# Router squares taken from residual chunks, router products spread over the projection, first expert item begun on two groups, state space end reordered, first projection weights in quarters

## The chip, the cores and the metric

The kernel runs on one core of a Trainium2 chip. The metric is the device time in microseconds (us) of one execution. A run's time is a little longer than the span of its profile, which goes from the first to the last instruction on the engines. Engines are named as in the profile: PE (TensorE, matmuls), DVE (VectorE), ACT (ScalarE), POOL (GpSimd) and SP (SyncE, which issues nearly all transfers). A float32 matmul appears on PE as two rows.

## The reference, cut to what matters

Two layers of a decoder are computed for 288 tokens (256 of a prompt, 32 samples), with 1024 channels. The change lies in the second one: from the end of the Mamba-2 state space mixer to the first of the experts.

```
y, state = ssd_chunked(x * dt, a, B, C, state0, chunk)        # 16 heads x 64, state 64
y = rms_normalize((y + d_skip * x) * silu(z))                  # in 4 groups of 256 channels
h = h + concat([o_hgrn, y * ssm_gain]) @ w_out                 # 1536 -> 1024
xn = rms_norm(h, norm_ffn_odd)
logits = xn @ w_router                                         # 8 experts
top_w, top_i = top_k(logits, 2)                                # softmax over the two
out = sum_e gate[e] * ((silu(xn @ we1[e]) * (xn @ we3[e])) @ we2[e])   # 3584 hidden
```

## The kernel before

Activations lie with channels on the 128 partitions, in 8 chunks of 128 channels by 288 tokens. The program is a row of stages. Each is a block in which every engine has its own hand-written list, with semaphores between the lists, and all engines meet at a stage's end. Nothing reorders: an instruction that waits holds up all that stands behind it on its engine.

**End of the state space stage (`stage_ssd`).** After the last product `y_prompt(7)`, PE computes the samples' state updates, `state_samples(0..7)`, each a product of 512 columns into PSUM banks 0 to 3 in turn, and `sum_squares(0..3)`, the sums for the group norm. DVE multiplies the old state by its decay (`decay_state`, line 2572) and then adds each product (`new_state`, line 2581). Update i from 4 on waits until `new_state` has emptied its bank. ACT squares the outputs and takes `root(0..3)`, two activations each.

**Output projection (`gemm_rows`, tag `_out_odd`).** 12 rows of weights in 6 halves of 2 rows (2048 columns in all per half). For each half, ACT rounds the weights (line 466, "hi"), and DVE subtracts to get the rest (line 472, "lo"). PE then makes for each of 8 output chunks m two pairs of hi products (lines 482 and 483) and two lo products (line 486), all of 288 columns; 48 such chunk steps of 6 products make the projection. `warm` (line 229) issues products whose result nobody uses. After a chunk of the last half, DVE adds it to `residual` (line 698), and `RouterHead.follow` has PE do the router products of a finished chunk (`score`, line 539, 8 columns) and its transpose (`turn`, line 548). ACT squares the transposed tokens in `square` (line 576), five of six tiles in this stage, the sixth in the next. DVE's `choose` turns the logits into the two chosen experts.

**Start of the experts (`stage_experts`).** PE counts ranks (line 3027) and items (line 3031), DVE takes the inverse norm from ACT and makes `at_first` (line 3078), and PE gathers the tokens of the first item for three groups of 32 slots (line 3042). DVE multiplies by the gain and transposes each group into `item_x` (line 3083). Then come `item(0)` to the last: 8 items in this profile. An item has 32 up blocks (line 2977: 12 matmuls of 448 columns each, a block is 0.918 MB) and 14 down blocks (line 2993: 24 matmuls, 1.049 MB). Of the first item six up blocks were loaded during the projection (`early_up`, which the rows call `odd_layer`). Up blocks go through a ring of 8 slots, down blocks through one of 7; SP issues a load when `up_used` or `down_used` says that a block has been used.

## Time and profile before

| what | us |
|---|---|
| median of 3 runs | 1584.04 |
| lowest and highest of them | 1583.19 and 1588.73 |
| the profiled execution | 1589.23 |
| its span | 1587.0 |
| end of the state space stage, from 617.59 to 631.43 | 13.84 |
| output projection, from 631.43 to 685.81 | 54.38 |
| routing, from 685.81 to the first item's product at 696.38 | 10.57 |
| experts, from 696.38 to the end | 890.6 |

The profiled execution is 5.2 us above the median, and its span 2.2 us below its own time. Places in the rows are in us from the start of the span. A row of a timeline merges like instructions that follow each other; x4 is their number.

### The profile page before, as it was taken

The numbers are of one execution on the slowest core, as the hardware profiler recorded it, in microseconds if no ns is written. First come the engines' busy times: TensorE is split into PE (matmuls) and PEld (weight loads), VectorE is DVE, ScalarE is ACT, GpSimd is POOL, SyncE is SP. The second block draws the span as 40 slices with busy tenths as digits, with TensorE's granted clock in tenths as the row PEclk, the third lists the DMA queues.
The fourth block names the chain that finished last, engine by engine and source line by source line (L and its number), as shares of the span: only waits on it lengthen the run. The fifth ranks groups of instructions, "written<-read, shape, count | busy, mean of one in ns | idle before, by whom it ended". The sixth has DMA issues, their size and how long they took to land.

```text
span 1587.0 us, 37321 instructions
## 1 busy us (share of the span) xinstructions
PE 1556.8 (98%) x16801; PEld 1144.1 (72%) x16801; DVE 532.5 (34%) x783; ACT 368.5 (23%) x550; POOL 43.9 (3%) x50
## 2 busy tenths in 40 slices
PE   9989999999999999999999999999999999999997
PEld 8976799999999965953576766745746537767456
DVE  6467556564559677552101101111011011011113
ACT  4346444443427467210000000000000000000001
POOL 0000000000000000000000000000000000000000
...
GB/s 356 192 240 192 144 141 190 163 160 133 164 154 167 152 165 40 263 275 419 338 395 414 416 405 414 414 407 416 403 415 414 406 416 416 406 417 414 407 414 227
DMA packets 144488, 479.46 MB, mean 302 GB/s; under 512 B 32184, under 2 KB 61632, under 8 KB 129747
## 3 DMA queue, kind: packets, MB, share of 16 engines
...
## 4 chain that ended last, share of the span: by engine, by line
PE 56%; DVE 0%; ACT 0%; issue 0%; DVEq 0%
PE ps L2977 36%; PE ps L2993 19%; PE ps L3042 0%; PE ps L3021 0%; PE ps L229 0%; PE ps L3002 0%; PE ps L3027 0%; PE ps L3009 0%; DVE act L3201 0%; DVE act L3191 0%; DVE tail_rows L3191 0%; DVEq L2870 0%; ACT xn_tokens L3257 0%; PE ps L3031 0%; ACT item_y L3242 0%
## 5 line engine op out<-in xcount | busy, mean ns | idle before, releaser
L2977 PE MATMUL ps<-up_ring,item_x 128*32 128x448 f32 x6000 | 567.3, 539 | 0.0
L2977 PEld LDWEIGHTS ps<-up_ring,item_x 128*32 128x32 f32 x6000 | 287.3, 110 | 273.5 <-issue 198.1
L2993 PE MATMUL ps<-down_ring,hid_t 128*32 128x256 f32 x5376 | 298.8, 379 | 1.1
L2993 PEld LDWEIGHTS ps<-down_ring,hid_t 128*32 128x32 f32 x5376 | 237.7, 110 | 62.1 <-issue 10.4
L3163 DVE TENSOR_TENSOR hid<-hid,ps 128x1344 f32<-128x1344 f32 x16 | 24.9, 1554 | 662.0 <-PE ps L2977 660.6
L472 DVE TENSOR_TENSOR w_lo_dense<-ring,w_hi_dense 128x2048 fp32r<-128x2048 f32 x54 | 123.6, 2291 | 96.0 <-ACT w_hi_dense L466 96.0
L466 ACT CAST w_hi_dense<-ring 128x2048 fp32r<-128x2048 f32 x54 | 102.9, 1906 | 93.7 <-PE ps L486 86.0
L3242 ACT COPY item_y<-ps 128x512 f32<-128x512 f32 x8 | 4.7, 585 | 428.8 <-PE ps L2993 428.8
L1558 PE MATMUL ps<-x_hi_dense,w_hi_dense 128*128 128x288 f32 x352 | 94.8, 299 | 1.8 <-PEq L1422 1.8
L1559 PE MATMUL ps<-x_lo_dense,w_hi_dense 128*128 128x288 f32 x352 | 94.6, 295 | 0.0
L3238 ACT ACTIVATE hid<-ps 128x1344 f32<-128x1344 f32 x16 | 20.7, 1291 | 269.6 <-PE ps L2977 269.5
L482 PE MATMUL ps<-x_hi_dense,w_hi_dense 128*128 128x288 f32 x272 | 73.8, 299 | 0.0
L483 PE MATMUL ps<-x_lo_dense,w_hi_dense 128*128 128x288 f32 x272 | 73.7, 295 | 0.0
L1558 PEld LDWEIGHTS ps<-x_hi_dense,w_hi_dense 128*128 128x128 f32 x352 | 66.2, 188 | 2.0 <-issue 2.0
L1559 PEld LDWEIGHTS ps<-x_lo_dense,w_hi_dense 128*128 128x128 f32 x352 | 66.1, 188 | 0.1
L482 PEld LDWEIGHTS ps<-x_hi_dense,w_hi_dense 128*128 128x128 f32 x272 | 51.3, 188 | 0.5 <-issue 0.5
L483 PEld LDWEIGHTS ps<-x_lo_dense,w_hi_dense 128*128 128x128 f32 x272 | 51.0, 188 | 0.0
L1563 PE MATMUL ps<-x_hi_dense,w_lo_dense 128*128 128x288 f32 x352 | 50.4, 296 | 0.0
L482 PE MATMUL ps<-x_hi_hidden,w_hi_dense 128*128 128x288 f32 x176 | 48.9, 293 | 0.7 <-PEq L1538 0.7
L483 PE MATMUL ps<-x_lo_hidden,w_hi_dense 128*128 128x288 f32 x176 | 48.9, 294 | 0.0
L1563 PEld LDWEIGHTS ps<-x_hi_dense,w_lo_dense 128*128 128x128 f32 x352 | 48.0, 188 | 0.0
L482 PE MATMUL ps<-x_hi_qkv,w_hi_qkv 128*128 128x288 f32 x176 | 47.8, 297 | 0.0
...
## 6 DMA issues: line engine op xcount, KB each, us to landing
...
down_ring<-in_we_dram SPq DMA_DIRECT2D x112, 1024.0 KB, 10.6
...
```

Source lines behind the costliest of these rows:

```text
L466: act.copy(self.view(self.hi, h), raw).then_inc(*self.hi_done.up())
L472: dve.tensor_tensor(self.view(self.lo, h), self.halves[h][2], self.view(self.hi, h).bitcast(F32), ALU.subtract)\
L482: pe.matmul(out, hi[:, c, cols], x[0][:, r, :], start=first and c == 0, stop=False)
L483: pe.matmul(out, hi[:, c, cols], x[1][:, r, :], start=False, stop=False)
L1558: pe.matmul(hidden.bank(m, w), hi[:, c, w, :], x[0][:, c, :], start=c == 0, stop=False)
L1559: pe.matmul(hidden.bank(m, w), hi[:, c, w, :], x[1][:, c, :], start=False, stop=False)
L1563: mm = pe.matmul(hidden.bank(m, w), lo[:, c, w, :], x[0][:, c, :], start=False, stop=c == DC - 1)
L2977: mm = pe.matmul(k.ps[32 * q:32 * q + 32, 3 * w + g, 0:FW], xg[:, c, g, :], block_of[:, q, :], start=c == 0, stop=c == DC - 1, skip_group_ ...
L2993: mm = pe.matmul(k.ps[32 * q:32 * q + 32, 6 + g // 2, 256 * (g % 2):256 * (g % 2) + 256], hidT[:, 2 * r + j, g, :], block_of[:, j, 256 * q ...
L3163: dve.tensor_tensor(hid[:, :, :], hid[:, :, :], k.ps[:, 3:6, 0:FW], ALU.mult).then_inc(mult_done, 1)
L3238: act.activation(hid[:, :, :], k.ps[:, 0:3, 0:FW], ACT.Silu).then_inc(silu_done, 1)
L3242: act.copy(y[:, 0:2, :], k.ps[:, 6, :].rearrange("p (g d) -> p g d", g=2)).then_inc(y_copied, 1)
```

## The change

Five things change. (1) At the state space end, PE's order is four updates, a sum, two updates, a sum, two updates, two sums and one unused product; updates 4 to 7 go to banks 5, 6, 0 and 1, and the last two sums reuse banks 4 and 7 after the roots have read them. DVE decays five of eight states ahead of `take(4)`. (2) The first half of the projection's weights is rounded and subtracted in quarters of 512 columns, and PE waits for a quarter instead of the half; 1 unused product stands ahead instead of 3. (3) Squares are taken by ACT from each residual chunk (288 columns, channels on the partitions), folded by DVE into one chunk, and summed over partitions by three one-column products; the inverse norm is computed within the projection's stage. (4) `follow` does one router product per chunk from m = 1 on; of the unused products, 4 become 1 at the projection's end and 2 become none in the routing. (5) The first item begins when two of the three groups are transposed: its first two blocks run group by group.

```diff
     def follow(self, pe, m):
-        if m == 4:
-            self.score(pe, 0)
-            self.score(pe, 1)
-            self.score(pe, 2)
-        elif m == 5:
-            self.score(pe, 3)
-            self.turn(pe, 0)
-            self.turn(pe, 1)
-        elif m == 6:
-            self.score(pe, 4)
-            self.turn(pe, 2)
-            self.score(pe, 5)
+        if m in (1, 2, 3):
+            self.score(pe, m - 1)
+        elif m in (4, 5, 6):
+            self.score(pe, m - 1)
+            self.turn(pe, m - 4)
         elif m == 7:
             self.turn(pe, 3)
             self.score(pe, 6)
             self.score(pe, 7)
+            self.sum(pe)
             for c in range(4, DC):
                 self.turn(pe, c)
-            self.k.warm(pe, 7, 4)
...
+            pe.wait_ge(*self.step.at(4))
+            self.k.warm(pe, 0, 1)
+    def sum(self, pe):
+        k = self.k
+        pe.wait_ge(*self.folded.at(DC - 1))
+        for i, (a, n) in enumerate(TILES):
+            mm = pe.matmul(k.ps[0:n, 7, i:i + 1], self.sq[:, 0, a:a + n], k.const("ones")[:, 0:1], start=i == 0, stop=True, skip_group_check=True)
+        mm.then_inc(*self.summed.up())
+    def square(self, act, c):
+        act.wait_ge(*self.added.at(c + 1))
+        act.activation(self.sq[:, c, :], self.k.residual[:, c, :], ACT.Square).then_inc(*self.squared.up())
+    def fold(self, dve, c):
+        dve.wait_ge(*self.squared.at(c + 1))
+        if c > 1:
+            dve.wait_ge(*self.folded.at(c - 1))
+        dve.tensor_tensor(self.sq[:, 0, :], self.sq[:, 0, :], self.sq[:, c, :], ALU.add).then_inc(*self.folded.up())
+    def take_mean(self, dve):
+        ps = self.k.ps
+        dve.wait_ge(*self.summed.at(1))
+        dve.tensor_scalar(self.rstd[:, 0:2], ps[:, 7, 0:2], 1.0 / D, EPS, ALU.mult, ALU.add).then_inc(*self.mean.up())
+        dve.tensor_scalar(self.rstd[0:TS, 2:3], ps[0:TS, 7, 2:3], 1.0 / D, EPS, ALU.mult, ALU.add).then_inc(*self.mean.up())
     def take(self, act):
-        act.wait_ge(*self.step.at(1))
+        for c in range(DC):
+            self.square(act, c)
         act.wait_ge(*self.turned.at(1))
         act.copy(self.rows[0][:, 0:512], self.turned_at(0, 0))
         act.copy(self.rows[1][:, 0:512], self.turned_at(1, 0))
-        squared = self.k.count("squared")
-        for u in range(2):
-            act.wait_ge(*self.turned.at(u + 1))
-            for i in range(3 - u):
-                if u or i:
-                    act.wait_ge(*squared.at(3 * u + i))
-                self.square(act, i, u).then_inc(*squared.up())
+        act.wait_ge(*self.mean.at(2))
+        act.activation(self.rstd, self.rstd, ACT.Ln).then_inc(*self.root.up())
+        act.wait_ge(*self.root.at(1))
+        act.activation(self.rstd, self.rstd, ACT.Exp, scale=-0.5).then_inc(*self.root.up())
...
+        self.take_mean(dve)
...
         sp_ = Split(k, weights or weight_parts(k, s, tag), halves + (in_odd_halves(k)[:1] if late else []), lambda h: half_done.at(h + 1),
-                    made=1 if hidden else 0, lo_made=1 if hidden else 0)
+                    made=1 if hidden else 0, lo_made=1 if hidden else 0, lead=PIECES - 1 if norm else 0, lo_lead=PIECES - 1 if norm else 0)
...
+        piece = lambda buf, p: buf[:, :, D // PIECES * p:D // PIECES * p + D // PIECES]
...
-                    k.warm(pe, 7, 3)
+                    k.warm(pe, 7, 1)
                 for h in range(len(halves)):
-                    sp_.await_hi(pe, h)
+                    if h or not norm:
+                        sp_.await_hi(pe, h)
                     for m in range(DC):
+                        lo_at = None
+                        if norm and h == 0:
+                            pe.wait_ge(*sp_.hi_done.at(m * PIECES // DC + 1))
+                            lo_at = sp_.lo_done.at(m * PIECES // DC + 1)
...
                         mm = sp_.products(pe, k.ps[:, m, 0:T], h, slice(P * m, P * m + P), range(2 * h, 2 * h + 2), x,
-                                          h == 0, h == last, source if m == 0 else None)
+                                          h == 0, h == last, source if m == 0 else None, lo_at)
...
+                    if norm and h == 0:
+                        act.wait_ge(*k.arrived(first))
+                        for p in range(PIECES):
+                            act.copy(piece(sp_.view(sp_.hi, 0), p), piece(halves[0][2], p)).then_inc(*sp_.hi_done.up())
+                    elif h >= sp_.made:
                         sp_.round_hi(act, h)
...
+                    if norm and h == 0:
+                        for p in range(PIECES):
+                            dve.wait_ge(*sp_.hi_done.at(p + 1))
+                            dve.tensor_tensor(piece(sp_.view(sp_.lo, 0), p), piece(halves[0][2], p), piece(sp_.view(sp_.hi, 0), p).bitcast(F32),
+                                              ALU.subtract).then_inc(*sp_.lo_done.up())
+                    elif h >= sp_.made:
                         sp_.take_lo(dve, h)
...
+                    if head and m >= 2:
+                        head.fold(dve, m - 1)
...
                 if head:
+                    head.fold(dve, DC - 1)
...
-        SUM_BANKS = (4, 7, 5, 6)
+        SUM_BANKS, STATE_BANKS = (4, 7, 4, 7), (0, 1, 2, 3, 5, 6, 0, 1)
...
-                    if i >= 4:
-                        pe.wait_ge(*n_["state_new"].at(i - 3))
+                    if i in (4, 5):
+                        pe.wait_ge(*n_["y_taken"].at(i + 3))
+                    if i >= 6:
+                        pe.wait_ge(*n_["state_new"].at(i - 5))
                     r = quarter(i % 4)
-                    pe.matmul(k.ps[:, i % 4, :], xs[r, 1, i // 4, :], bbd[r, i // 4, :, :], start=True, stop=True)\
+                    pe.matmul(k.ps[:, STATE_BANKS[i], :], xs[r, 1, i // 4, :], bbd[r, i // 4, :, :], start=True, stop=True)\
                       .then_inc(*n_["state_dot"].up())
...
-                        pe.wait_ge(*n_["y_taken"].at(5 + g))
+                        pe.wait_ge(*n_["root"].at(2 * g - 3))
...
-                state_samples(0)
-                state_samples(1)
+                for i in range(4):
+                    state_samples(i)
                 sum_squares(0)
-                state_samples(2)
-                state_samples(3)
+                state_samples(4)
+                state_samples(5)
                 sum_squares(1)
+                state_samples(6)
+                state_samples(7)
                 sum_squares(2)
-                for i in range(4, 6):
-                    state_samples(i)
                 sum_squares(3)
-                for i in range(6, 8):
-                    state_samples(i)
+                pe.wait_ge(*n_["state_new"].at(5))
+                k.warm(pe, 5, 1)
...
+                dve.wait_ge(*n_["st_turned"].at(NB))
+                dve.wait_ge(*n_["ebc_exp"].at(1))
+                for j in range(5):
+                    decay_state(j)
                 take(4)
...
                 take(6)
-                dve.wait_ge(*n_["st_turned"].at(NB))
-                decay_state(0)
-                decay_state(1)
+                decay_state(5)
                 take(7)
-                for j in range(2, 8):
-                    decay_state(j)
+                decay_state(6)
+                decay_state(7)
...
-                for j in range(4):
+                for j in range(6):
                     square(j)
                 root(0)
-                square(4)
-                square(5)
-                root(1)
                 square(6)
                 square(7)
+                root(1)
                 root(2)
                 root(3)
...
+                def open_item():
+                    pe.wait_ge(silu_done, 1)
+                    for g, chunks in ((0, range(2)), (1, range(2)), (2, range(2))):
+                        if g == 0:
+                            pe.wait_ge(*half_x.at(3))
+                        if g == 2:
+                            pe.wait_ge(xg_ready, 1)
+                        for c in chunks:
+                            if g == 0:
+                                pe.wait_ge(up_loaded[c], 16)
+                            block_of = head.early_up[:, UP_COLS * c:UP_COLS * c + UP_COLS].rearrange("p (q n) -> p q n", q=4)
+                            for q in range(4):
+                                mm = pe.matmul(k.ps[32 * q:32 * q + 32, g, 0:FW], xg[:, c, g, :], block_of[:, q, :],
+                                               start=c == 0, stop=False, skip_group_check=True)
+                            if g == 2:
+                                mm.then_inc(up_used, 1)
                 def item(i, opening=False):
-                    pe.wait_ge(xg_ready, i + 1)
+                    if opening:
+                        open_item()
+                    else:
+                        pe.wait_ge(xg_ready, i + 1)
                     for n in range(2):
                         for w in range(2):
-                            pe.wait_ge(mult_done if w else silu_done, i * 2 + (n + 1))
-                            for c in range(DC):
+                            if not opening or n + w:
+                                pe.wait_ge(mult_done if w else silu_done, i * 2 + (n + 1))
+                            for c in range(2 if opening and n + w == 0 else 0, DC):
...
-                k.warm(pe, 2, 2)
                 pe.wait_ge(*slotted.at(3))
...
-                dve.wait_ge(*summed.at(1))
...
                 dve.wait_ge(*ranked.at(1))
...
                 then(dve.scalar_tensor_tensor(spot0[:, :], ranks[:, :, 0], 1.0, chosen[:, :, 0], ALU.add, ALU.mult))
-                dve.wait_ge(*inverted.at(2))
...
-                head.square(act, 2, 1).then_inc(*summed.up())
                 act.copy(tail[:, 0:512], head.turned_at(2, 0)).then_inc(*copied.up())
-                act.wait_ge(*averaged.at(1))
-                act.activation(rstd[:, :], rstd[:, :], ACT.Ln).then_inc(*inverted.up())
-                act.wait_ge(*inverted.at(1))
-                act.activation(rstd[:, :], rstd[:, :], ACT.Exp, scale=-0.5).then_inc(*inverted.up())
...
```

PE, from the last product of the state space to the first chunk of the projection, before (L2453 updates, L2465 sums, L229 unused products; `ring` and `act` are the names of reused buffers):

```order
L2453 MATMUL ps<-b_by_sample,x_samples 128x512 x2
L2465 MATMUL ps<-act,core 128x288 x2
L2453 MATMUL ps<-b_by_sample,x_samples 128x512 x2
L2465 MATMUL ps<-act,core 128x288 x4
L2453 MATMUL ps<-b_by_sample,x_samples 128x512 x2
L2465 MATMUL ps<-act,core 128x288 x2
L2453 MATMUL ps<-b_by_sample,x_samples 128x512 x2
L2384 UNCONDITIONAL_BRANCH
L640 UNCONDITIONAL_BRANCH
L229 MATMUL ps<-ones_wide,core 128x288 x3
L482 MATMUL ps<-x_hi_hgrn_out,w_hi_out_odd 128x288
```

The same place now (L2489 updates, L2501 sums):

```order
L2489 MATMUL ps<-b_by_sample,x_samples 128x512 x4
L2501 MATMUL ps<-act,core 128x288 x2
L2489 MATMUL ps<-b_by_sample,x_samples 128x512 x2
L2501 MATMUL ps<-act,core 128x288 x2
L2489 MATMUL ps<-b_by_sample,x_samples 128x512 x2
L2501 MATMUL ps<-act,core 128x288 x4
L229 MATMUL ps<-ones_wide,core 128x288
L2418 UNCONDITIONAL_BRANCH
L657 UNCONDITIONAL_BRANCH
L229 MATMUL ps<-ones_wide,core 128x288
L482 MATMUL ps<-x_hi_hgrn_out,w_hi_out_odd 128x288
```

The second sum has gone behind two more updates, no update stands behind the last sum any more, and two of the unused products have gone.

PE in the last half of the projection, before, from the last products of chunk 4 on (L539 router products, L548 transposes):

```order
L483 MATMUL ps<-x_lo_out_odd,w_hi_out_odd 128x288
L486 MATMUL ps<-x_hi_out_odd,w_lo_out_odd 128x288 x2
L539 MATMUL ps<-act,residual 128x8 x2
L539 MATMUL ps<-act,residual 32x8
L539 MATMUL ps<-act,residual 128x8 x2
L539 MATMUL ps<-act,residual 32x8
L539 MATMUL ps<-act,residual 128x8 x2
L539 MATMUL ps<-act,residual 32x8
L482 MATMUL ps<-x_hi_out_odd,w_hi_out_odd 128x288
L483 MATMUL ps<-x_lo_out_odd,w_hi_out_odd 128x288
L482 MATMUL ps<-x_hi_out_odd,w_hi_out_odd 128x288
L483 MATMUL ps<-x_lo_out_odd,w_hi_out_odd 128x288
```

Now, from the last products of chunk 1 on (L543 router products):

```order
L483 MATMUL ps<-x_lo_out_odd,w_hi_out_odd 128x288
L489 MATMUL ps<-x_hi_out_odd,w_lo_out_odd 128x288 x2
L543 MATMUL ps<-act,residual 128x8 x2
L543 MATMUL ps<-act,residual 32x8
L482 MATMUL ps<-x_hi_out_odd,w_hi_out_odd 128x288
L483 MATMUL ps<-x_lo_out_odd,w_hi_out_odd 128x288
L482 MATMUL ps<-x_hi_out_odd,w_hi_out_odd 128x288
L483 MATMUL ps<-x_lo_out_odd,w_hi_out_odd 128x288
L489 MATMUL ps<-x_hi_out_odd,w_lo_out_odd 128x288 x2
L543 MATMUL ps<-act,residual 128x8 x2
L543 MATMUL ps<-act,residual 32x8
L482 MATMUL ps<-x_hi_out_odd,w_hi_out_odd 128x288
```

Three router products in a row have become one behind each chunk.

PE from the end of the projection to the first item, before:

```order
L548 MATMUL ps<-core,residual 32x128
L229 MATMUL ps<-ones_wide,core 128x288 x4
L629 UNCONDITIONAL_BRANCH
L2964 UNCONDITIONAL_BRANCH
L3027 MATMUL ps<-act,core 128x8 x6
L3031 MATMUL ps<-act,core 128x8 x3
L229 MATMUL ps<-ones_wide,core 128x288 x2
L3042 MATMUL ps<-act,at_first 32x256 x8
L3042 MATMUL ps<-tail_rows,at_first 32x256 x4
L3042 MATMUL ps<-act,at_first 32x256 x8
L3042 MATMUL ps<-tail_rows,at_first 32x256 x4
L3042 MATMUL ps<-act,at_first 32x256 x8
```

Now (L3081 ranks, L3085 counts, L3095 gathering products):

```order
L552 MATMUL ps<-core,residual 32x128
L229 MATMUL ps<-ones_wide,core 128x288
L646 UNCONDITIONAL_BRANCH
L2997 UNCONDITIONAL_BRANCH
L3081 MATMUL ps<-act,core 128x8 x6
L3085 MATMUL ps<-act,core 128x8 x3
L3095 MATMUL ps<-act,at_first 32x256 x8
L3095 MATMUL ps<-tail_rows,at_first 32x256 x4
L3095 MATMUL ps<-act,at_first 32x256 x8
L3095 MATMUL ps<-tail_rows,at_first 32x256 x4
L3095 MATMUL ps<-act,at_first 32x256 x8
L3095 MATMUL ps<-tail_rows,at_first 32x256 x4
```

Five of six unused products have gone from this place, and gathering follows the counts at once.

## Rows read from the trace of the kernel before

**Rows 1.** The page of the profile, its first line: the span.

```profile
span 1587.0 us, 37321 instructions
```

**Rows 2.** Waits after 700 us: who for whom, us in total, times, longest.

```profile
PE ps L3021 <- ACT item_y L3243: 0.9, 1, 0.9
```

**Rows 3.** Timeline of PE in the experts: start, length, what, count.

```profile
696.38 13.74 PE L2977 MATMUL ps<-odd_layer,item_x 128*32 128x448 f32 x144 [1.03 <-DVE item_x L3083]
...
1027.61 72.39 PE L2977 MATMUL ps<-up_ring,item_x 128*32 128x448 f32 x768
```

**Rows 4.** Stretches: length, busy us and count by engine, clock, DMA share, GB/s.

```profile
697.00:740.00 43.00, 43.00 (x446) 15.96 (x442) 16.60 (x59) 2.80 (x3) 0.00 (x0) 1.00 1.02 413
```

**Rows 5.** Timeline of PE, end of the state space stage and next start.

```profile
617.59 1.13 PE L2453 MATMUL ps<-b_by_sample,x_samples 32*128 32x512 f32 x4
...
621.49 2.21 PE L2465 MATMUL ps<-act,core 128*128 128x288 f32 x8
624.40 1.72 PE L2453 MATMUL ps<-b_by_sample,x_samples 32*128 32x512 f32 x4 [0.71 <-DVE ring L2581]
626.05 1.74 PE L2465 MATMUL ps<-act,core 128*128 128x288 f32 x4
...
631.43 3.22 PE L229 MATMUL ps<-ones_wide,core 128*128 128x288 f32 x6 [1.64 <-PEq L2384]
634.03 0.85 PE L482 MATMUL ps<-x_hi_hgrn_out,w_hi_out_odd 128*128 128x288 f32 x1
```

**Rows 6.** Timeline of DVE there; in brackets idle time and what ended it.

```profile
612.62 0.42 DVE L2564 TENSOR_TENSOR mixed_out<-ps,odd_layer 128x256 f32<-128x256 f32 x1 [3.52 <-PE ps L2419]
...
619.93 3.69 DVE L2572 TENSOR_TENSOR ring<-ring,ebc 128x512 f32<-128x512 f32 x6
623.66 3.68 DVE L2581 TENSOR_TENSOR ring<-ring,ps 128x512 f32<-128x512 f32 x6
629.82 1.28 DVE L2581 TENSOR_TENSOR ring<-ring,ps 128x512 f32<-128x512 f32 x2 [2.49 <-PE ps L2453]
```

**Rows 7.** Timeline of ACT: a root, the weight rounding, a 512-column copy.

```profile
627.82 0.41 ACT L2700 ACTIVATE act<-ps 128x288 f32<-128x288 f32 x1 [2.80 <-PE ps L2465]
...
631.40 3.70 ACT L466 CAST w_hi_out_odd<-ring 128x2048 fp32r<-128x2048 f32 x2 [2.70 <-PEq L2384]
...
680.92 0.58 ACT L581 COPY act<-ps 128x512 f32<-128x512 f32 x1 [17.74 <-PE ps L548]
```

**Rows 8.** Stretches again, columns as in group 4: three places at reduced clock.

```profile
631.00:640.00 9.00, 8.50 (x38) 7.30 (x39) 6.77 (x8) 4.38 (x3) 0.00 (x0) 0.67 0.90 181
671.00:681.00 10.00, 10.00 (x74) 9.59 (x73) 2.02 (x5) 0.08 (x1) 0.00 (x0) 0.83 0.00 0
...
686.00:697.00 11.00, 9.97 (x102) 4.93 (x105) 4.76 (x15) 2.76 (x8) 0.00 (x0) 0.84 0.94 365
```

**Rows 9.** Timeline of PE from the router products to the first gathering products.

```profile
671.35 2.07 PE L539 MATMUL ps<-act,residual 128*128 128x8 f32 x18
...
683.33 2.11 PE L229 MATMUL ps<-ones_wide,core 128*128 128x288 f32 x8
685.81 1.48 PE L3027 MATMUL ps<-act,core 128*128 128x8 f32 x12 [0.38 <-PEq L629]
...
687.81 2.02 PE L229 MATMUL ps<-ones_wide,core 128*128 128x288 f32 x4
689.76 1.90 PE L3042 MATMUL ps<-act,at_first 128*32 128x256 f32 x16
```

**Rows 10.** Timeline of DVE: two additions of a chunk, the choice's last step, slots.

```profile
669.17 0.46 DVE L698 TENSOR_TENSOR residual<-residual,ps 128x288 f32<-128x288 f32 x1 [0.34 <-PE ps L486]
669.96 0.46 DVE L698 TENSOR_TENSOR residual<-residual,ps 128x288 f32<-128x288 f32 x1 [0.33 <-PE ps L486]
...
684.25 0.18 DVE L610 SCALAR_TENSOR_TENSOR act<-act,core 128x24 f32<-128x24 f32 x1
...
687.60 0.81 DVE L3078 TENSOR_SCALAR at_first<-slots,first_spot,rstd_tokens 128x96 f32<-128x96 f32 x3
```

38 lines of the change are left out of this document (16 added, 22 removed).

## The prediction, made before the changed kernel ran

> **What bounds the kernel now.** I read the span first [rows 1], then where the time lies: the experts take 890 of 1587 us. In the list of waits after 700 us the reader is to see what PE waits for: one wait of 0.9 us for ACT, at the very end, and none for a transfer [rows 2]. PE is also as fast on the six blocks that were loaded long before (144 rows in 13.74 us, 2.29 us a block) as on ring blocks (768 rows in 72.39 us, 2.26 a block) [rows 3]. So PE's pace sets the experts, and none of it changes. The transfers are close behind: an item moves 32 x 0.918 + 14 x 1.049 = 44.0 MB in 890.6 / 8 = 111.3 us, so 396 GB/s, where the queues show a share of 1.02 and 413 GB/s [rows 4]. What is left is a plain rule: whatever brings the first item forward brings the end forward by as much, while transfers keep up. The change works in the 79 us before the first item, and I go through it by place.
>
> **1. End of the state space.** The tail is a shuttle between PE and DVE. Updates 4 and 5 (624.40) wait for DVE, sum 3 follows, updates 6 and 7 come last, and DVE adds them only at 629.82, having sat idle 2.49 us; it ends at 631.10 and the stage 0.3 us later [rows 5, 6]. Now PE's list has no wait for DVE that matters: after 617.59 there are 8 updates (1.13 us for two, so 0.565 each) and 4 sums (2.21 us for two, 1.1 each), 8 x 0.565 + 4 x 1.1 = 8.9 us, so 626.5 [rows 5]. ACT's last root is two activations of 0.41 us behind it [rows 7], with hand-over 627.4. DVE must have its part by then. Five decays go ahead of `take(4)`; six take 3.69 us, so 0.61 each and 3.1 us for five, and DVE sits idle 3.52 us there [rows 6], waiting for PE. That is their cover, with 0.4 us to spare; without it they would push back `take(4)` and with it all of PE's last four y products by up to 3.1 us. Left behind are decays 5, 6 and 7: `take(7)` at about 619.0, the last decay ends near 620.6, eight additions at 0.61 end at 625.5 [rows 6]. PE's sums are then the last to end, and the next stage starts at 627.4 + 0.3 = 627.7 instead of 631.43: **-3.7 us**. Bounds: nothing, if some wait stays, and -5.6, if only DVE counted (625.8).
>
> **2. Start of the projection.** Today three unused products, six rows, take 3.22 us at half clock, and the first real product is at 634.03, 2.6 us into the stage [rows 5]; the first hi rounding took 1.9 of them (two in 3.70) [rows 7]. Now PE needs a quarter, 512 columns. No row shows that shape; the nearest is the copy of 512 columns, 0.58 us [rows 7]. The lo quarter is a fourth of DVE's pass over the half, about 0.65, and is asked for only 0.5 us after the hi one. Each quarter feeds two chunk steps of 0.79 us (the distance of two additions [rows 10]), so no later quarter is waited for. First product 0.6 us in: **-2.0 us** (bounds -1.3, behind a slow unused product, and -2.1).
>
> **3. The clock.** Three stretches show the granted clock below 1.0: 0.67 of 9 us, 0.83 of 10, 0.84 of 11 [rows 8]. With levels of 2.4 and 1.2 GHz, 1 - c of a stretch is half the time at the lower level, and that is what the level costs when PE is busy. First, 2 x 0.33 x 9 = 5.9 us from 631 on. PE had idled before it for 1.64 us and, before that, between small pieces of work [rows 5]. Of this the products from 634.03 run 2.9 us at half speed, which costs 1.4. The new tail is dense to 626.9 and PE idles about 1.3 us until 628.3, so I expect the clock to hold: **-1.4 us** (bound +1.5: it falls later and takes six us of products). Second, 3.4 us within 671 to 681. Here PE did not idle at all: it did 18 rows of router products, 2.07 us with 8 columns each, then one chunk, then more of them [rows 8, 9]. It costs 1.7. Spread out, each such piece of 0.69 us stands beside a full chunk of 0.79: **-1.7 us** (bounds 0 and -1.7). The Trainium skill, page "TensorE: Matmul & The Clock Gate", Part 1, says that idling drops TensorE to the low level and sustained busyness lifts it. Its count of idle time alone would make this second term nothing, since PE was busy without a break, and the trace contradicts that reading.
>
> **4. End of the projection.** The eight squares, seven folds and the sum are hidden: ACT sat idle for 17.74 us ahead of its copies there [rows 7], and DVE has 0.79 + 0.69 us per chunk for an addition of 0.46 [rows 10] and a fold that I take to cost the same; the last fold is done 3 x 0.46 = 1.4 us after the last chunk, by when PE does a transpose and two router products (1.5). If that cover is gone, 0.45 more. What ends the stage today are four unused products, 683.33 + 2.11 = 685.44 [rows 9]. One of four saves 1.6, but DVE's choice ended at 684.43 [rows 10] and now carries two small operations and the wait for three one-column products, some 0.5 us: 684.9. **-0.5 us** (bounds 0 and -1.0).
>
> **5. Routing and first item.** The gathering products wait for `at_first` (687.60 + 0.81 = 688.4) but stand behind the unused ones until 689.76 [rows 9, 10]: -1.3. Squares and roots are gone from this stage, but ranks (1.48 us) were the later of the two anyway. The item waits 1.03 us for the third group after PE's last gathering product [rows 3]; the second is ready by then, and PE's work on two groups of two blocks, 2/3 of 4.6 us, covers the third's transposition: -1.0. Against this stands the clock. Today it is at the low level for 2 x 0.16 x 11 = 3.5 us here [rows 8], though six unused products stood around. Now a single one is left between the last chunk and the gathering products, about 8 us filled with one- to 128-column work like that of 671.35. I take 6 us at the low level instead of 3.5, so +1.3. **-1.0 us** (bounds -3.1, if the level never falls, and +3.6, if ranks, counts and all gathering run at half: 4.6 + 9.6 us against 10.6).
>
> **Sum**: -3.7 - 2.0 - 1.4 - 1.7 - 0.5 - 1.0 = -10.3 us. The profiled execution (1589.2) would become 1578.9. It stood 5.2 us above the median and the terms don't depend on that, so against the median I say 1584.04 - 10.3 = 1573.7.
>
> **Transfers.** They move with the stage, but the item starts a little earlier in it. Loads already queued at 685.8 are 2 up and 4 down blocks, 6.0 MB or 14.6 us at 413 GB/s. The first block behind them is needed 8 x 2.29 = 18.3 us into the item, some 28 us into the stage. Ten us are spare, so this costs nothing.
>
> **The rivals.** (a) The low clock persists: it is at half from the projection's end into the item, since the unused products that fed it are gone, and the item's own products don't lift it soon. For it speaks the fall at 674 with a busy PE; against it that four-fold gathering products brought it back at about 691. Each us of it costs half a us: with 9 us more at half, 4.5, **1578.2**. It would have to last over 20 us longer than my 6 to use up the gain, and 36 to make the kernel slower by 8 us: **1592**. The Trainium skill's page "TensorE: Matmul & The Clock Gate", Part 1, speaks for a quick return, since sustained work should lift the clock. (b) The clock falls at the projection's start, as before, but now under products instead of unused ones: term 3's first part becomes +1.5 instead of -1.4, **1576.6**. (c) The clock holds everywhere: term 5 is -3.1, **1571.6**. (d) The experts are set by transfers, which start with the stage: then term 5 is lost, **1574.7**; against it, PE's waits [rows 2]. (e) The reordering gains nothing, because some wait stays in the tail and the first products go at the old pace: only terms 4 and 5 and the second clock term stay, -3.2, **1580.8**. (f) The second fall of the clock has nothing to do with the order of the router products and stays: **1575.4**; for it speaks only that the spread-out products are as many as before. By the rule on idling of that page of the Trainium skill it would have had no cause in them either.
>
> **How the numbers follow.** A measurement of this kernel tells 0.5% from no change, 7.9 us: below 1576.1 is faster. Chances: my forecast 0.40, (c) 0.18, (d) 0.04, (f) 0.05, (b) 0.13, (a) 0.12 without and 0.03 with the slower end, (e) 0.05. Faster are the first four, 0.67, and about half of (b), 0.06; slower is 0.03; the rest, 0.24, is within 0.5%. The range runs from beyond (c), where terms 1 and 2 are also at their bounds (1569.5), to just past (a) (1579.5); what it leaves out is (e), the slower end and some of (a).
>
> **What would show it.** The next stage's first row near 627.7 and the first hi product 0.6 us behind; no fall of the clock between there and the last chunk; the start of the experts about 9.3 us earlier than 685.8; the first item's first row 9.5 to 10.5 us behind that, without a wait for `item_x`. I am wrong if PE waits in the tail for DVE, if DVE's decays delay `take(4)`, if PE waits for quarters, or if the first six blocks take clearly more than 13.7 us.

## The result and the profile after

The changed kernel takes 1580.77 us in the median of 7 runs (1578.41 to 1585.04); 7 runs of the kernel before beside it take 1588.73 (1583.19 to 1592.02). The ratio is 0.9957, interval 0.9939 to 0.9975: 0.43% or 6.8 us faster, where 10.3 us, and a time of 1573.7 us, were forecast. Two further sets of runs of the same kernel give 0.9963 [0.9947, 0.9980] and 0.9949 [0.9928, 0.9969]. The profiled execution takes 1580.99 us, at a mean granted clock of 0.993.

PE at the end of the state space stage, after, against [rows 5]:

```profile
620.98 1.14 PE L2489 MATMUL ps<-b_by_sample,x_samples 32*128 32x512 f32 x8
622.65 1.24 PE L2501 MATMUL ps<-act,core 128*128 128x288 f32 x4 [0.53 <-ACT act L2733]
...
627.10 2.21 PE L2501 MATMUL ps<-act,core 128*128 128x288 f32 x8
629.15 0.65 PE L229 MATMUL ps<-ones_wide,core 128*128 128x288 f32 x2
630.54 0.72 PE L229 MATMUL ps<-ones_wide,core 128*128 128x288 f32 x2 [0.74 <-PEq L2418]
631.18 0.40 PE L482 MATMUL ps<-x_hi_hgrn_out,w_hi_out_odd 128*128 128x288 f32 x1
...
631.91 0.53 PE L489 MATMUL ps<-x_hi_hgrn_out,w_lo_out_odd 128*128 128x288 f32 x2
```

No wait for DVE is left in the tail. The next stage's first row stands 9.56 us behind the first update (it was 13.84), and the first hi product 0.64 us behind that (it was 2.60). The first lo product (631.91) comes 1.37 us into the stage.

DVE and ACT there, after, against [rows 6, 7]:

```profile
622.72 1.28 DVE L2608 TENSOR_TENSOR ring<-ring,ebc 128x512 f32<-128x512 f32 x2
624.04 4.87 DVE L2617 TENSOR_TENSOR ring<-ring,ps 128x512 f32<-128x512 f32 x8
631.16 2.50 DVE L713 TENSOR_TENSOR w_lo_out_odd<-ring,w_hi_out_odd 128x512 fp32r<-128x512 f32 x4 [2.25 <-ACT w_hi_out_odd L690]
```

```profile
629.79 0.44 ACT L2739 ACTIVATE act<-act 128x288 f32<-128x288 f32 x1
630.51 2.18 ACT L690 CAST w_hi_out_odd<-ring 128x512 fp32r<-128x512 f32 x4 [0.28 <-PEq L2418]
```

DVE's eight additions end at 628.91, ACT's last root at 630.23: ACT ends the stage. A hi quarter is 2.18 / 4 = 0.55 us, a lo quarter 0.63.

PE from the last chunk to the item, after, against [rows 9, 3]:

```profile
674.90 1.37 PE L543 MATMUL ps<-act,residual 128*128 128x8 f32 x12
676.25 0.76 PE L576 MATMUL ps<-core,mixed_out 128*128 128x1 f32 x6
676.94 1.53 PE L552 MATMUL ps<-core,residual 128*128 128x128 f32 x12
678.31 0.65 PE L229 MATMUL ps<-ones_wide,core 128*128 128x288 f32 x2
679.46 1.48 PE L3081 MATMUL ps<-act,core 128*128 128x8 f32 x12 [0.50 <-PEq L646]
680.79 0.81 PE L3085 MATMUL ps<-act,core 128*128 128x8 f32 x6
682.11 1.70 PE L3095 MATMUL ps<-act,at_first 128*32 128x256 f32 x16 [0.51 <-DVE at_first L3127]
...
684.75 1.94 PE L3095 MATMUL ps<-act,at_first 128*32 128x256 f32 x16
...
690.50 7.45 PE L3011 MATMUL ps<-odd_layer,item_x 128*32 128x448 f32 x48
697.77 9.19 PE L3031 MATMUL ps<-odd_layer,item_x 128*32 128x448 f32 x96
706.79 4.68 PE L3031 MATMUL ps<-up_ring,item_x 128*32 128x448 f32 x48
```

The item's first row has no wait any more. But its first two blocks, 48 rows, take 7.45 us, where the 96 rows of the next four take 9.19. The stretches say why (columns as in [rows 4, 8]; this is after):

```profile
631.00:640.00 9.00, 9.00 (x67) 8.66 (x66) 7.18 (x10) 6.10 (x8) 0.00 (x0) 1.00 1.01 203
...
666.00:676.00 10.00, 10.00 (x86) 9.70 (x84) 5.21 (x13) 2.96 (x7) 0.00 (x0) 1.00 0.08 30
682.00:696.00 14.00, 13.89 (x104) 3.88 (x108) 6.79 (x22) 0.00 (x0) 0.00 (x0) 0.51 0.97 403
696.00:707.00 11.00, 11.00 (x120) 3.48 (x116) 8.55 (x31) 0.22 (x1) 0.00 (x0) 1.00 0.80 283
```

The clock holds where it had fallen at 631 and at 671, and is at the low level for 2 x 0.49 x 14 = 13.7 us from 682.4 on, through nearly all gathering products and into the item, with PE busy 13.89 of 14 us.

**The same code, another execution.** The changed kernel was profiled again (c0 below). PE there:

```profile
678.15 1.48 PE L3081 MATMUL ps<-act,core 128*128 128x8 f32 x12 [0.50 <-PEq L646]
679.48 0.81 PE L3085 MATMUL ps<-act,core 128*128 128x8 f32 x6
680.80 1.07 PE L3095 MATMUL ps<-act,at_first 128*32 128x256 f32 x16 [0.50 <-DVE at_first L3127]
...
685.49 4.72 PE L3011 MATMUL ps<-odd_layer,item_x 128*32 128x448 f32 x48
690.03 9.20 PE L3031 MATMUL ps<-odd_layer,item_x 128*32 128x448 f32 x96
```

```profile
677.00:688.00 11.00, 10.00 (x122) 4.92 (x124) 5.80 (x21) 2.01 (x4) 0.00 (x0) 1.00 0.82 314
688.00:702.00 14.00, 14.00 (x152) 4.81 (x148) 11.33 (x40) 0.22 (x1) 0.00 (x0) 1.00 1.01 409
```

Ranks, counts and the waits are the same to 0.01 us, and the clock doesn't fall between the tail and the sixth block: 16 gathering rows in 1.07 us instead of 1.70 to 1.94, routing 7.34 us instead of 11.04, first six blocks 13.56 instead of 16.29. One kernel differs from itself by 6.4 us, as much as the whole change is worth, so that one profile can't price a clock term.

**All profiles in one table.** Each row is one execution; us. Tail: from the first state update to the next stage's first ACT row. First: from there to the first hi product. Proj.: to the last lo product of the last chunk. End: to the ranks. Rout.: to the item's first row. Six: the first six blocks. Low: where the granted clock is at the low level between the tail and the sixth block, start and length.

| kernel | tail | first | proj. | end | rout. | six | sum | low |
|---|---|---|---|---|---|---|---|---|
| before | 13.81 | 2.63 | 46.04 | 5.74 | 10.57 | 13.56 | 92.35 | 626.6: 10.2, 674.4: 3.4, 688.1: 3.4 |
| b0 (before) | 12.38 | 1.95 | 47.29 | 9.16 | 10.56 | 13.56 | 94.90 | 680.6: 13.7, 697.7: 3.4 |
| after | 9.53 | 0.67 | 43.12 | 5.16 | 11.04 | 16.29 | 85.81 | 682.4: 13.7 |
| c0 (after) | 9.54 | 0.67 | 43.11 | 5.15 | 7.34 | 13.56 | 79.37 | none |
| e2 (after) | 9.54 | 0.67 | 42.74 | 5.15 | 7.34 | 13.56 | 79.00 | none |
| a1 | 9.53 | 0.67 | 43.14 | 5.15 | 9.42 | 13.55 | 81.46 | 682.9: 3.4 |
| a2 | 9.53 | 0.67 | 42.73 | 6.40 | 11.27 | 15.78 | 86.38 | 686.6: 13.7 |
| a3 | 9.53 | 0.68 | 43.15 | 6.41 | 7.84 | 13.55 | 81.16 | none |
| c1 | 9.53 | 0.67 | 44.17 | 5.74 | 13.07 | 15.25 | 88.43 | 671.8: 3.4, 685.4: 13.7 |
| c2 | 12.36 | 1.95 | 46.28 | 5.15 | 8.92 | 13.55 | 88.21 | 638.8: 3.4, 690.0: 3.4 |
| c3 | 9.54 | 0.67 | 42.65 | 5.15 | 10.42 | 15.22 | 83.65 | 682.4: 10.2 |
| d1 | 9.53 | 0.68 | 43.12 | 5.16 | 8.93 | 13.55 | 80.97 | 679.8: 3.4 |
| d2 | 9.53 | 1.95 | 45.77 | 5.15 | 11.27 | 15.89 | 89.56 | 637.5: 3.4, 688.7: 13.7 |
| d3 | 9.53 | 0.67 | 42.73 | 5.15 | 12.42 | 14.95 | 85.45 | 679.0: 13.7 |
| d4 | 9.54 | 0.66 | 42.72 | 5.15 | 11.01 | 16.33 | 85.41 | 680.9: 13.7 |
| e1 | 9.53 | 0.67 | 42.74 | 5.15 | 7.36 | 13.55 | 79.00 | none |
| e3 | 9.53 | 0.67 | 43.16 | 5.15 | 10.01 | 13.55 | 82.07 | 677.9: 3.4 |
| e4 | 12.36 | 0.67 | 44.22 | 5.74 | 10.51 | 13.55 | 87.05 | 675.4: 3.4, 689.1: 3.4 |

One more distance, from the next stage's first ACT row to the first lo product, is 4.28 us in all four executions with whole halves (before, b0, c2, d2) and 1.40 us in all 14 with quarters. It is the same in before, where the clock was low there, and in b0, where it was not.

### The profile page after: what moved, and what is told of

The parts are those of the page before. It is cut to its first block, busy times and chain, and to the rows that moved or that the text cites. A ratio compares the mean times of both kernels' runs of the same rounds, so it can differ in the third digit from the quotient of the medians.

```text
span 1578.8 us, 37320 instructions
## 1 busy us (share of the span) xinstructions
PE 1550.4 (98%) x16795; PEld 989.6 (63%) x16795; DVE 534.6 (34%) x793; ACT 368.5 (23%) x549; POOL 43.9 (3%) x50
## 3 DMA queue, kind: packets, MB, share of 16 engines
HBM read 463.57 MB, written 13.55 MB: 302 GB/s over the span
## 4 chain that ended last, share of the span: by engine, by line
PE 55%; DMA 1%; DVE 1%; SPq 0%; ACT 0%; DVEq 0%; issue 0%
PE ps L3031 36%; PE ps L3047 17%; DMA xn_tokens<-y_rows 1%; PE ps L3095 1%; PE ps L3011 0%; DVE act L3227 0%; DVE act L3232 0%; PE ps L3075 0%; PE ps L3056 0%; PE ps L3081 0%; PE ps L3063 0%; SPq L2957 0%; DVE act L3250 0%; DVE tail_rows L3232 0%; DVE act L3240 0%; DVE tail_rows L3240 0%
## 5 line engine op out<-in xcount | busy, mean ns | idle before, releaser
L3031 PEld LDWEIGHTS ps<-up_ring,item_x 128*32 128x32 f32 x6000 | 196.2, 110 | 364.3 <-issue 363.1
L3047 PE MATMUL ps<-down_ring,hid_t 128*32 128x256 f32 x5376 | 291.6, 379 | 0.0
L3047 PEld LDWEIGHTS ps<-down_ring,hid_t 128*32 128x32 f32 x5376 | 176.1, 110 | 116.5 <-issue 3.9
## 6 DMA issues: line engine op xcount, KB each, us to landing
up_ring<-in_we_dram SPq DMA_DIRECT2D x250, 896.0 KB, 10.3
```

The lines of the kernel that those rows point to most:

```text
L3031: mm = pe.matmul(k.ps[32 * q:32 * q + 32, 3 * w + g, 0:FW], xg[:, c, g, :], block_of[:, q, :], start=c == 0, stop=c == DC - 1, skip_group_ ...
L3047: mm = pe.matmul(k.ps[32 * q:32 * q + 32, 6 + g // 2, 256 * (g % 2):256 * (g % 2) + 256], hidT[:, 2 * r + j, g, :], block_of[:, j, 256 * q ...
```

## The experiments

Theory S (structure): what the change removes or adds of work decides, and the clock follows the order of the instructions, so unused products in the routing keep it up. Theory V (variation): the clock's falls come and go from execution to execution, and the one profile of before credited falls as if they were fixed. A rival to both is that opening on two groups, or the old burst of router products, brings the long stretch. Below, "clock" is the mean granted clock over a kernel's timed runs.

**a1: two unused products back in the routing.**

```diff
                                  start=w == 0, stop=w == NW - 1)
+                k.warm(pe, 2, 2)
```

> The changed kernel with the two unused products in the routing put back (behind the counts, ahead of the gathering products). Theory A (the clock: what is missing from the forecast is the stretch at 1.2 GHz from the routing into the first item, 13.7 us in the changed kernel against 3.5 us before): the two products cost 1.0 to 2.0 us ahead of the gathering, the low level ends within about 5 us, the first six blocks take 13.6 to 14.5 us instead of 16.3, and from the start of the experts' stage to the seventh block it takes 24.5 to 26 us instead of 27.3; 1.5 to 3 us faster than the changed kernel, a ratio to before of about 0.994. Theory B (the opening by groups is slower by itself, or the blocks wait for transfers): the first six blocks stay at 16.3 us and the two products only add 1 us; 28 us and more, ratio 0.996 or above.

1579.20 us (7 runs), ratio 0.9963 [0.9949, 0.9977], clock 0.9950. The stretch is 3.4 us here, the item undisturbed, as theory A had it. But the ratio isn't the expected 0.994; it is no lower than that of the change as made.

**a2: four unused products at the projection's end instead of one.**

```diff
-            self.k.warm(pe, 0, 1)
+            self.k.warm(pe, 0, 4)
```

> The changed kernel with four unused products instead of one at the end of the projection's stage. Theory A: PE becomes the last engine of that stage, which ends 1.5 us later; the clock falls one step later or not at all before the gathering, the low level lasts 3 to 8 us instead of 13.7 and the first six blocks take 13.6 to 15 us; from the last chunk of the projection to the seventh block 30 to 32.5 us against 32.2 in the changed kernel. Theory B: the six blocks stay at 16.3 us and the sum is 33.7 us.

1582.49 us (12 runs), 0.9966 [0.9945, 0.9987], clock 0.9936. The end is 1.25 us longer, and 13.7 us are low all the same:

```profile
682.09 2.11 PE L229 MATMUL ps<-ones_wide,core 128*128 128x288 f32 x8
684.49 1.48 PE L3081 MATMUL ps<-act,core 128*128 128x8 f32 x12 [0.30 <-PEq L646]
685.82 0.81 PE L3085 MATMUL ps<-act,core 128*128 128x8 f32 x6
687.14 1.94 PE L3095 MATMUL ps<-act,at_first 128*32 128x256 f32 x16 [0.50 <-DVE at_first L3127]
```

Full products 2 us ahead of the ranks don't hold the clock in this execution. Theory A had 3 to 8 us low and at most 15 us for the six blocks, which took 15.78.

**a3: both.**

> The changed kernel with all six unused products at these two places, as before the change. Theory A: the clock behaves as before the change (about 3.5 us low, back before the second group's gathering), the first six blocks take 13.6 to 13.8 us, and from the last chunk of the projection to the seventh block it takes about 28.5 us (29.6 before the change, less the 1.0 us that the item no longer waits for its third group); about 3.5 us faster than the changed kernel. Theory B: 16.3 us for the six blocks and 35 us in all, slower than the changed kernel by 2 to 3 us.

1578.62 us (11 runs), 0.9965 [0.9949, 0.9981], clock 0.9953; no fall, 1.25 us lost at the end. The 3.5 us that theory A expected over the changed kernel are not in the times.

**b0: the kernel before, once more.**

> The kernel before, unchanged, for a second profile of it. The first profiles show two differences outside the change: the changed kernel reached the end of the state space 3.4 us later, and its experts behind the seventh block took 5.1 us less (down products of an item in 36.4 us instead of 37.5). Theory V (varies from execution to execution): this profile differs from the first one in at least one of them by over 1 us. Theory K (belongs to the kernel): 617.6 and 877.1 us within 0.5 us, with down products at 37.5 us.

1594.40 us, clock 0.989 in this one run. The projection starts at full clock here. PE there, before again:

```profile
637.42 1.69 PE L229 MATMUL ps<-ones_wide,core 128*128 128x288 f32 x6 [1.64 <-PEq L2384]
639.35 0.40 PE L482 MATMUL ps<-x_hi_hgrn_out,w_hi_out_odd 128*128 128x288 f32 x1 [0.23 <-ACT w_hi_out_odd L466]
...
641.67 0.53 PE L486 MATMUL ps<-x_hi_hgrn_out,w_lo_out_odd 128*128 128x288 f32 x2 [1.53 <-DVE w_lo_out_odd L472]
```

The six unused rows take 1.69 us, where [rows 5] have 3.22, and the tail 12.38 us instead of 13.81: the old tail and first product held 1.43 + 0.68 us of low clock in the profile that the forecast read. But PE then waits 1.53 us for the lo half, which it did not in the forecast's profile. In exchange the clock falls from 680.6, for 13.7 us, over the end of the projection with its four unused products. The experts behind the sixth block take 872.28 us here and 872.0 to 874.3 in all others, but 877.06 in the forecast's profile: 2.7 to 5.1 us more than in the others, so that at least half of its 5.2 us above the median lay there. Theory V holds: 617.6 and 877.1 us don't belong to the kernel.

**c0: the changed kernel again.**

> The changed kernel, unchanged, on the same chip as the next three. Theory A (clock): it shows again about 13.7 us at 1.2 GHz from the routing into the first item, in most executions; six blocks take 15 to 16.5 us; mean granted clock of its runs near 0.993 against 0.995 for the kernel before; ratio 0.995 to 0.997. Theory V (the long low stretch was an accident of one execution): the low stretch is 3.4 us or none here, six blocks 13.6 us, ratio 0.993.

1579.83 us (12 runs), 0.9963 [0.9947, 0.9980], clock 0.9942. Shown above. The profile is as theory V said, the ratio and the mean clock over 12 runs as theory A did. The profiled execution was the second fastest of these 12, and that of e2 the fastest of its 12.

**c1: only the state space end and the quarters** (parts 1 and 2 of the change, the rest as before).

> Of the change only the state space end and the weights in quarters (with one unused product instead of three ahead of the projection); router, squares, routing and item opening as before. Theory A: the work of these two parts is worth 4.3 + 2.0 = 6.2 us, whatever the clock does, and with the six unused products of the router's end in place the clock is low for no longer than before: 6 to 8.5 us faster, ratio 0.9945 to 0.996, so this half of the change alone gives all that the whole change gives. Rival (the router's parts carry the gain): ratio above 0.9975.

1581.41 us (12 runs), 0.9969 [0.9954, 0.9985], clock 0.9939. Theory A had at most 0.996. Its routing has the old unused products and still a long stretch, the one such case behind the ranks; that of b0 ends 1.5 us ahead of them.

**c2: only the router parts** (parts 3 to 5, the rest as before).

> Of the change only the router's parts: squares from chunks, spread router products, fewer unused products at the projection's end and in the routing, item opened on two groups; state space end and whole halves of weights as before. Theory A: 0.6 us at the projection's end, 0 to 1.7 from the clock in the last half, against 0.5 + 2.7 us lost from the routing to the seventh block: between 1 us faster and 2.5 us slower, ratio 0.9995 to 1.0015; low clock of 10 us and more there. Rival (forecast right for these parts): 4.2 us faster, ratio 0.9973.

1585.38 us (12 runs), 0.9987 [0.9972, 1.0002], clock 0.9939. Theory A had 0.9995 to 1.0015 and 10 us or more at the low clock; there are 3.4. The two halves add: 0.31% + 0.13% against 0.37% for c0 beside them.

**c3: the changed kernel with the old order of router products in `follow`.**

```diff
-        if m in (1, 2, 3):
-            self.score(pe, m - 1)
-        elif m in (4, 5, 6):
-            self.score(pe, m - 1)
-            self.turn(pe, m - 4)
+        if m == 4:
+            self.score(pe, 0)
+            self.score(pe, 1)
+            self.score(pe, 2)
+        elif m == 5:
...
```

> The changed kernel with the router products of chunks 0 to 5 at their old places (three in a row behind chunk 4, then three more with the transposes). Theory F (the forecast's step: the row of router products makes the clock fall within the last half): the clock falls between 668 and 678 us, the projection takes 1 to 1.7 us longer. Theory G (the fall there depends on where the execution stands, and on more than these rows): the projection takes 43.1 us as in the changed kernel, and its time is the same within 1 us.

1579.86 us (12 runs), 0.9970 [0.9953, 0.9987], clock 0.9930. The burst of 18 router rows is back, and the clock holds over it in this execution (PE, then the stretch):

```profile
666.40 2.06 PE L543 MATMUL ps<-act,residual 128*128 128x8 f32 x18
```

```profile
664.00:676.00 12.00, 12.00 (x102) 11.57 (x100) 6.04 (x17) 4.48 (x10) 0.00 (x0) 1.00 0.25 102
```

A long stretch from 682.4 (10.2 us) is there too, so it doesn't need the spread products. The projection is as short as in the changed kernel: theory G, in this execution.

**d1: one unused product behind the counts** (as a1, with `k.warm(pe, 2, 1)`).

> The changed kernel with one unused product behind the counts, where PE waits 0.5 us for DVE anyway. So far the same changed kernel showed 13.7 us at 1.2 GHz in one profile and none in another, with no difference in its order: theory L says that the full-clock length of each stretch belongs to the kernel (routing 7.3 us, six blocks 13.56) and the low stretches fall by where an execution stands. L: routing at full clock 7.3 to 7.5 us, mean granted clock of the runs 0.994 to 0.996, 1 us faster than the changed kernel at most. Rival (one product is enough to hold the clock): no low stretch, all runs at 0.996 and above, 2 to 4 us faster.

1577.27 us (6 runs), 0.9927 [0.9901, 0.9954], clock 0.9950; 3.4 us low. Theory L allowed 1 us over the changed kernel, its rival 2 to 4 without any stretch; the time is the rival's, the trace and the clock are L's.

**d2: the changed kernel with the first half whole.**

```diff
-    nblocks, PIECES = -(-total // 4), 4
+    nblocks, PIECES = -(-total // 4), 1
```

> The changed kernel with the first half of the projection's weights rounded whole instead of in quarters, still one unused product ahead. L: tail 9.53 us as before; first product 1.9 to 2.0 us into the stage instead of 0.67, plus up to 1 us of waiting for the lo part; 1.3 to 2.3 us slower than the changed kernel. Rival (the two unused products taken away were what cost the time): first product within 1 us.

1587.72 us (12 runs), 0.9993 [0.9975, 1.0011], clock 0.9911, the lowest of all kernels with several runs. PE at the start of the projection, d2:

```profile
633.49 0.72 PE L229 MATMUL ps<-ones_wide,core 128*128 128x288 f32 x2 [0.74 <-PEq L2418]
635.41 0.40 PE L482 MATMUL ps<-x_hi_hgrn_out,w_hi_out_odd 128*128 128x288 f32 x1 [1.20 <-ACT w_hi_out_odd L690]
...
637.74 0.85 PE L489 MATMUL ps<-x_hi_hgrn_out,w_lo_out_odd 128*128 128x288 f32 x2 [1.53 <-DVE w_lo_out_odd L713]
```

PE waits 1.20 us for the whole hi half and 1.53 for the lo one, and the clock falls at 637.5. All that the change gains is lost, where theory L had 1.3 to 2.3 us: the mean is 6.9 us, give or take 2.2, above that of the changed kernel's 31 runs. Of this 2.9 us are the later first lo product (4.28 us into the stage, not 1.40), and the rest fits the mean clock.

**d3: the first item opened on three groups** (its wait for the third group moved ahead of the first).

```diff
-                            pe.wait_ge(*half_x.at(3))
-                        if g == 2:
```

> The changed kernel with the first item begun only when all three groups are transposed. L: routing 1.0 us longer (8.35 at full clock), six blocks 13.56; 1 us slower. Rival (the opening on two groups delays the blocks by its order): six blocks shorter than 13.55 us.

1579.83 us (8 runs), 0.9949 [0.9924, 0.9975], clock 0.9930. The wait is back:

```profile
689.81 6.13 PE L3009 MATMUL ps<-odd_layer,item_x 128*32 128x448 f32 x48 [1.07 <-issue]
```

But routing and six blocks together take 27.37 us, and 27.33 in after with the same 13.7 us low. In d3 the stretch begins 1.3 us nearer to the ranks and holds 1.25 us in which PE idles, in after none, so it cost less. The 1.07 us are seen in the trace; no time shows them.

**d4: none of the three unused products** (at the tail, ahead of the projection, behind the last chunk).

> The changed kernel without any of its three unused products (state space end, projection's start, projection's end). L: stretches at full clock as in the changed kernel or 0.1 to 0.5 us shorter, mean granted clock lower (0.991 to 0.993), 0 to 3 us slower. Rival (unused products of this size don't reach the clock): mean clock as in the changed kernel, 0.994, and the same time or 0.5 us faster.

1581.46 us (12 runs), 0.9958 [0.9938, 0.9978], clock 0.9925; the projection starts at full clock without any of them. The mean is 1.6 us, give or take 2.5, above that of the changed kernel, so no time shows what they are worth; the mean clock is as low as theory L said.

**e1, e2, e3: one, no and three unused products behind the counts, on one chip.**

> The changed kernel with one unused product of two groups of columns behind the counts of the routing, a second time. Theory A (an unused product in the routing shortens the stretch at 1.2 GHz): no more than 3.4 us of the clock low from the router product to the first item's sixth block, routing 8.9 us or less, first six blocks 13.55 us, and a ratio to the kernel before about 0.002 below that of the changed kernel run beside it (about 0.993 against 0.9955), with a mean clock at least 0.001 above it. Theory B (the stretch varies from execution to execution whatever stands there): the low stretch may be 0 to 13.7 us here, and both the ratio and the mean clock agree with those of the changed kernel within 0.001.

> The changed kernel itself, as the partner of the other two. Theory A: 10 to 13.7 us at 1.2 GHz in routing and first item in most executions, so a mean clock near 0.9935 and a ratio of about 0.9955. Theory B: any length between 0 and 13.7 us, and a ratio no different from that with one or three unused products.

> The changed kernel with three unused products behind the counts. Theory A: the clock holds as with one (3.4 us low at most), the first six blocks take 13.55 us, and the routing is about 0.5 to 1 us longer than with one, as two more products stand ahead of the rank product: a ratio 0.0003 to 0.0006 above that with one. Theory B: the routing is that much longer and nothing is gained: a ratio 0.0005 above that of the changed kernel.

| | median (runs) | ratio | mean | clock |
|---|---|---|---|---|
| e1, one | 1575.62 (10) | 0.9925 [0.9902, 0.9948] | 1576.38 | 0.9956 |
| e2, none | 1578.68 (12) | 0.9949 [0.9928, 0.9969] | 1579.09 | 0.9938 |
| e3, three | 1576.08 (9) | 0.9932 [0.9907, 0.9957] | 1576.19 | 0.9968 |

Times and clocks come out as theory A said, though the means of e1 and e2 differ by 2.7 us, give or take 2.7. The profiles of the pair don't tell it: neither e1 nor e2 has a fall, and theory A had a long stretch for e2. What the product costs they do show. PE in e1:

```profile
678.97 1.48 PE L3081 MATMUL ps<-act,core 128*128 128x8 f32 x12 [0.50 <-PEq L646]
680.30 0.81 PE L3085 MATMUL ps<-act,core 128*128 128x8 f32 x6
680.97 0.73 PE L229 MATMUL ps<-ones_wide,core 128*128 128x288 f32 x2
681.63 1.07 PE L3096 MATMUL ps<-act,at_first 128*32 128x256 f32 x16
```

It fills the wait of 0.50 us for `at_first`: from the ranks to the gathering are 2.66 us, and 2.65 in c0 without it. With three it is 5.31 us (e3, the product rows at 1.2 GHz).

**e4: the kernel before with only the quarters.**

> The kernel before with only the projection's weights for the first half loaded in quarters and one unused product instead of three ahead of them; the state-space end, the router and the routing as before. Theory Q (the quarters alone let the projection start at full clock): tail 12.4 us at full clock, first product 0.7 instead of 1.95 to 2.6 us, no stretch at 1.2 GHz at the projection's start, 1.3 us faster by the work and up to 4 us where the fall is avoided: a ratio of 0.9975 to 0.9990. Rival (the fall belongs to the state-space end, with its last products behind the reads): a stretch of 3.4 to 3.7 us at 1.2 GHz stays at the projection's start, and the ratio is 0.999 or more.

1584.39 us (12 runs), 0.9992 [0.9969, 1.0014], clock 0.9923. PE, e4, then the stretch:

```profile
635.88 0.72 PE L229 MATMUL ps<-ones_wide,core 128*128 128x288 f32 x2 [1.64 <-PEq L2402]
636.52 0.40 PE L482 MATMUL ps<-x_hi_hgrn_out,w_hi_out_odd 128*128 128x288 f32 x1
```

```profile
631.00:641.00 10.00, 8.36 (x46) 5.77 (x45) 8.00 (x13) 5.52 (x8) 0.00 (x0) 1.00 0.45 91
```

With the old tail and its idle 1.64 us the clock holds, once PE no longer waits for the halves: the trace speaks for theory Q. The ratio is the rival's (0.999 or more), but its interval holds 0.9982, the 2.9 us by which the first lo product comes earlier, as well as nothing.

## Why the prediction was right or wrong

**The work was forecast well.** The forecast's terms hold parts that are work and parts that are clock; taken apart with b0, c0 and e2:

| term | forecast | of it work | work measured |
|---|---|---|---|
| 1 end of the state space | -3.7 | -2.3 | -2.85 (12.38 to 9.53) |
| 2 and first part of 3, start of the projection | -3.4 | -2.8 | -2.88 (4.28 to 1.40, to the first lo product) |
| second part of 3, rest of the projection | -1.7 | 0 | +0.2 (42.1 and 42.2 to between 42.1 and 42.5, at full clock) |
| 4 end of the projection | -0.5 | -0.5 | -0.59 (5.74 to 5.15) |
| 5 routing, first item | -1.0 | -2.3 | -1.5 (8.87 to 7.34, six blocks equal) |
| sum | -10.3 | -7.9 | -7.6 |

The work in term 1 is the forecast less the 1.43 us that b0 showed to be low clock, and 8.87 is 10.57 less half of the 3.4 us low in it. Term 2 and the first part of term 3 belong together. The forecast gave 2.0 us to an earlier first hi product and 1.4 to the clock. But what came next in the profile of before was this:

```profile
635.68 0.85 PE L486 MATMUL ps<-x_hi_hgrn_out,w_lo_out_odd 128*128 128x288 f32 x2
```

That is 4.28 us behind the stage's first ACT row, as in b0 at full clock: the whole lo half of DVE set it, and the low clock cost only what came behind it, 0.6 us. The forecast counted no wait for the lo half, so its two terms had the right sum by luck. In term 5 the third group's wait went as forecast (1.03 us in [rows 3], none after). The unused products were mis-sized: -1.3 us was read from rows at half clock. By the full-clock rows 2.65 us lie between ranks and gathering without them, and about 3.1 before (3.95 less half of the 1.8 us low between them), so -0.4. The bound of -3.1 us for that term doesn't follow from its own parts (-1.3, -1.0 and half of 3.5 us make -4.1, and rival (c) 1570.6); c0 measured -3.2.

The timed runs agree with the work alone. The means of before (113 runs) and after, c0 and e2 (31 runs) are 1586.66 and 1579.43 us: 7.2 us apart, give or take 1.4.

**The step that failed** is the clock: the second part of term 3 (-1.7) and 0.6 of its first part, the clock's +1.3 in term 5, and the 1.43 us of low clock that term 1 held unseen. Of the profiled execution the forecast said that "the terms don't depend on that". At least half of its 5.2 us above the median did lie elsewhere, in the experts, but the terms depended on where the clock fell in it: together they counted 1.4 + 0.6 + 1.7 - 1.3 = 2.4 us as gained clock. The timed runs show no such gain: the mean clock is 0.9939 over 113 runs of before and 0.9938 over 31 of after. Within a kernel 0.001 of it goes with 1.2 us, so the clock's part of the difference is about nothing. The second step is the 0.9 us too many for the unused products in term 5. And the base was low: of the 7.1 us between 1573.7 and 1580.77, 2.6 are the three runs' median of before against the mean of 113, 3.1 the gain (10.3 against 7.2), and 1.3 the seven runs of after, whose mean is 1580.71.

**Term 3, by place.** At the projection's start the forecast's expectation held: the clock falls in 3 of 4 executions with whole halves (in before already in the tail) and in 0 of 14 with quarters. Of the cause it had named only a part. d2, with the new tail, falls, and e4, with the old one, doesn't, which speaks for the waits for the halves and against the tail; b0 has those waits too, and held, so they don't decide it alone. In the last half, the clock falls in 4 of 5 executions with the old bursts of router products, and in 0 of 13 with them spread. That speaks against rival (f), by counts alone; c3 shows that the burst needn't do it. Since the mean clocks are equal, what these two places saved must have been given back; the routing is where the profiles show it.

**Term 5, the clock.** "I take 6 us at the low level instead of 3.5" was 13.7 in the profiled execution, rival (a) in place and kind, and nothing in c0 and e2. Between the ranks and the sixth block, over the 18 profiles: with unused products in the routing (10), 3.4 us seven times, none twice, 13.7 once, a mean of 3.8; without (8), 13.7 five times, 10.2 once and none twice, a mean of 9.8. The difference, 6.1 us low, is worth 3 us at half speed. The mean clocks say the same: 0.9950 to 0.9968 in the five kernels that are the changed one with such products (a1, a3, d1, e1, e3), 0.9925 to 0.9938 in the five that lack them and keep the quarters (the changed kernel over its 31 runs, a2, c3, d3, d4). The times say it less clearly. e1 and d1 (16 runs) have a mean of 1576.6 us and e3 1576.2, but a1 and a3 1578.9 and 1579.5; after, c0 and e2 (31 runs) have 1579.4. The 43 runs with products are ahead by 1.8 us, give or take 1.5; part of what a1, a3 and e3 miss is the work of their own products, 0.4, 1.8 and 1.0 us. So dropping the two products with the others most likely cost 1 to 3 us, and a single one, at 0.02 us, most likely brings them back. One product isn't shown to be better than two or three: the kernels ran beside different runs of before. Rival (c), the clock that holds everywhere, was there in two of three executions of the changed kernel, which were among the fastest of their runs, so the rivals were no alternatives between kernels but between executions.

The Trainium skill, page "TensorE: Matmul & The Clock Gate", Part 1, warns that one kernel shows different numbers of slow products from run to run. It says so of a kernel's start; the pair after and c0, 13.7 us against none in the same code, shows it in the middle. The Trainium skill's rule there that idling lowers the level could account for d2, but b0 idled as long (1.64, 0.23 and 1.53 us) without a fall there, and it doesn't account for after: there PE was busy for all but 0.51 us from the ranks until 682.4.

**The other rivals.** (b) and (d) are out: no fall at the start in 14 executions, and PE's pace behind the sixth block is unchanged (768 rows of ring blocks in 72.34 us). (e) has the measured number, 1580.8, by chance: the tail lost 2.85 us, and the first products came earlier. Transfers were no bound: the first ring block at 706.79 follows without a wait.

**Open.** What decides in a given execution whether the clock falls in the routing isn't known. The falls there begin 1.6 to 3.6 us behind the first ranks, whatever the absolute time. Why c1 had a long one in spite of four rows of unused products isn't explained. Nor is why whole halves cost the changed kernel 6.9 us (d2), while quarters alone gained the kernel before only 1.6 in the mean, give or take 2.6 (e4). Each variant has one profile, so that what a trace shows of its clock is one execution's. The best kernel seen is e1 (or d1, the same code): 0.9925 and 0.9927 against 0.9957, 0.9963 and 0.9949 for the change as made.
